# Last block of a two-layer model on one core: expert layer gathered by halves of the experts, and last tiles done one column half after the other

## What is computed

```python
def moe_swiglu(h, router, w_gate, w_up, w_down):
    ht = h.reshape(B * T, D)
    probs = jax.nn.softmax((ht @ router).astype(F32), axis=-1)
    top_p, top_i = lax.top_k(probs, TOP_K)                  # TOP_K = 2
    top_p = top_p / jnp.sum(top_p, axis=-1, keepdims=True)
    gates = jnp.sum(jax.nn.one_hot(top_i, N_EXPERTS, dtype=F32) * top_p[..., None], axis=1)
    out = jnp.zeros_like(ht)
    for e in range(N_EXPERTS):                              # 8 experts, hidden width 1536
        out = out + gates[:, e:e + 1] * swiglu(ht, w_gate[e], w_up[e], w_down[e])
    return out.reshape(B, T, D)
```

## Time and profile before

| | us |
|---|---|
| runs (3): lowest, median, highest | 1679.25, 1679.99, 1686.19 |
| the profiled execution: its own time | 1679.47 |
| its span | 1677.7 |
| TensorE busy in the span | 1612.0 |
| VectorE, ScalarE busy | 1166.4, 962.9 |
| weights and constants read, result written | 336.66 MB, 1.10 MB |

### The profile page before, as it was taken

How to read it: one execution, slowest core, us unless ns; L and a number is a source line. 1 busy time by engine, 2 the same in 40 slices (tenths; PEclk the granted TensorE clock), 3 DMA queues, 4 the chain that set the end, 5 groups by cost and what they waited for, 6 DMA issues and landing times.

```text
span 1677.7 us, 30052 instructions
## 1 busy us (share of the span) xinstructions
PE 1612.0 (96%) x11794; PEld 1435.0 (86%) x11794; DVE 1166.4 (70%) x1346; ACT 962.9 (57%) x1256; POOL 26.5 (2%) x37
## 2 busy tenths in 40 slices
PE   7999999999989999999999999999899999999997
PEld 6988999899879999899799998998678888888885
DVE  5677666644557666786755455867559888999885
ACT  6566455555565555754543445634357777777774
POOL 0000000000000000100000000200000000000000
PEclk9999999999999999999999999999889999999999
DMA  7535555434325555442345553631339999999993
GB/s 267 187 113 180 196 179 196 151 151 176 126 77 201 182 193 179 151 156 77 126 164 188 188 187 126 185 117 60 152 125 375 346 343 364 359 358 357 349 361 119
DMA packets 48225, 339.15 MB, mean 202 GB/s; under 512 B 5776, under 2 KB 5952, under 8 KB 8192
## 3 DMA queue, kind: packets, MB, share of 16 engines
q1 hardware_dynamic: 46064, 330.94, 53.4%
q0 software_dynamic: 2064, 6.83, 1.4%
HBM read 336.66 MB, written 1.10 MB: 201 GB/s over the span
## 4 chain that ended last, share of the span: by engine, by line
PE 53%; DVE 4%; ACT 3%; issue 1%; ACTq 0%; DVEq 0%
PE PS L1557 16%; PE PS L826 8%; PE PS L1575 8%; PE PS L1628 8%; PE PS L1645 4%; PE PS L1213 2%; PE PS L1512 1%; PE PS L1587 1%; DVE MWL L2463 1%; DVE ARENA L2846 1%; PE PS L1540 1%; PE PS L903 1%; ACT MWH L1785 1%; PE PS L1527 0%; ACT HN L1721 0%
## 5 line engine op out<-in xcount | busy, mean ns | idle before, releaser
L3050 DVE TENSOR_TENSOR EWL<-W,EWH 128x2048 fp32r<-128x2048 f32 x144 | 329.1, 2290 | 44.3 <-ACT EWH L2258 44.3
L2258 ACT ACTIVATE EWH<-W 128x2048 fp32r<-128x2048 f32 x144 | 276.2, 1919 | 67.5 <-PE PS L1575 36.7
L1628 PE MATMUL PS<-HTH,WH 128*128 128x256 f32 x1056 | 298.1, 282 | 5.3 <-DVE HTL L2435 5.3
L2458 DVE TENSOR_TENSOR WL<-W,WH 128x2048 fp32r<-128x2048 f32 x99 | 226.3, 2289 | 103.0 <-ACT WH L1767 102.0
L1628 PE MATMUL PS<-HTH,WL 128*128 128x256 f32 x1056 | 297.8, 282 | 0.0
L1628 PE MATMUL PS<-HTL,WH 128*128 128x256 f32 x1056 | 297.6, 282 | 0.0
L2463 DVE TENSOR_TENSOR MWL<-W,MWH 128x1024 fp32r<-128x1024 f32 x138 | 173.1, 1259 | 127.3 <-ACT MWH L1785 124.9
L1785 ACT ACTIVATE MWH<-W 128x1024 fp32r<-128x1024 f32 x138 | 144.7, 1055 | 167.8 <-PE PS L826 167.7
L1767 ACT ACTIVATE WH<-W 128x2048 fp32r<-128x2048 f32 x99 | 189.3, 1915 | 60.2 <-PE PS L1628 32.7
L1628 PEld LDWEIGHTS PS<-HTH,WH 128*128 128x128 f32 x1056 | 199.9, 189 | 7.0 <-issue 5.9
L1628 PEld LDWEIGHTS PS<-HTL,WH 128*128 128x128 f32 x1056 | 200.0, 189 | 1.0
(11 more groups left out here) (331 smaller groups left out, 2804.9 us busy)
## 6 DMA issues: line engine op xcount, KB each, us to landing
W<-in_weights SPq DMA_DIRECT2D x312, 1024.0 KB, 5.0
ARENA<-rows_m POOLq DMA_DIRECT2D x8, 192.0 KB, 5.4
ARENA<-rows_m POOLq DMA_DIRECT2D x2, 768.0 KB, 10.3
CS<-in_consts POOLq DMA_DIRECT2D x3, 403.0 KB, 4.3
X<-in_x SPq DMA_DIRECT2D x2, 512.0 KB, 3.6
out<-X SPq DMA_DIRECT2D x1, 1024.0 KB, 4.0
PR<-in_params SPq DMA_DIRECT2D x1, 830.0 KB, 7.7
CS<-in_consts POOLq DMA_DIRECT2D x2, 403.5 KB, 4.3
```

The lines of the kernel that those rows point to most:

```text
L1628: ins = mm(PS[b][:, c * 256:(c + 1) * 256], wt[:, sl, o:o + P], ht[:, kk, :], start=(kk == 0 and n == 0), stop=(kk == KC - 1 and n == 2))
L2258: A(EWH[tile % SPLIT][:, :], tile_ap(w0 + tile), ACT.Copy).then_inc(sem("moe_hi"), 1)
L2458: TT(WL[:, j % SPLIT, :], tile_ap(t), WH[:, j % SPLIT, :].bitcast(F32), SUB).then_inc(lo_done, 2)
L3050: TT(EWL[tile % SPLIT][:, :], tile_ap(w0 + tile), EWH[tile % SPLIT][:, :].bitcast(F32), SUB).then_inc(sem("moe_lo"), 1)
```

## The change

It has four parts. **Norms:** in front of mixers the table load goes behind the three splits; in front of FFNs the Silu load goes behind the evictions of the transposed rows. **Last tiles:** `out_last_tile` and the last `down` of an FFN finish one bank of y after the other. **Norm 7, router, gather:** HN is split a token tile at a time inside norm 7, two of four residual matmuls go between the transposes of the two token tiles, the router's first row of matmuls waits for each bank of HT by itself, SELR is made and the gather is run for experts 0 to 3 and then 4 to 7, evictions alternate between ScalarE and VectorE, and the transposes of SELR go behind chunks 2 to 5 of the second half. HNH and HNL move to other memory, so the first two expert tiles are split earlier. **End:** the last down tile is split ahead of the last group's Silu, the last turn goes inside the down before it, the last down, YH, YL and scatter run by column halves, the four copies are shared out, and the result leaves in four DMAs of 256 KB, with the branch for more tokens ahead of them.

```diff
@@ SyncE
-        for b in range(4):
-            await_free_of(sp, ("y", last_resid, b))
         if last_resid == "moe":
             with sp.If(more_tokens(sp) > 0):
...
-        sp.dma_start(out_dram.rearrange("b (t p) d -> p (b t) d", p=P), X[:, :, :]).then_inc(s_out, 16)
-        sp.wait_ge(s_out, 16)
+        out_tiles = out_dram.rearrange("b (t p) d -> p (b t) d", p=P)
+        for b in (0, 2, 1, 3):
+            await_free_of(sp, ("y", last_resid, b))
+            t, cols = b // 2, slice((b % 2) * 512, (b % 2 + 1) * 512)
+            sp.dma_start(out_tiles[:, t, cols], X[:, t, cols]).then_inc(s_out, 16)
+        sp.wait_ge(s_out, 64)
@@ TensorE, norm
                     if t == NT - 1:
                         done(ins, ("norm", n, b))
+                if n == 7 and t == 0:
+                    residual_in(moe_name[0], (0, 1))
@@ TensorE, out_last_tile
             for tt in range(NT):
-                for k, c in enumerate(chunks):
-                    for hf in range(2):
+                for hf in range(2):
+                    for k, c in enumerate(chunks):
                         ins = products(PS[2 * tt + hf][:, :], False, name, h + k, slice(hf * 512, (hf + 1) * 512), c,
                                        slice(tt * P, (tt + 1) * P), False, k == 1)
...
@@ TensorE, router
-            hT_ready(7)
...
             for t in range(NT):
-                for k in range(KC):
+                for j, b in enumerate((0, 2, 1, 3)):
+                    if t == 0:
+                        await_free_of(pe, ("norm", 7, b))
+                    for i, k in enumerate(NORM_CHUNKS[b]):
...
-            residual_in(moe_name[0])
+            residual_in(moe_name[0], (2, 3))
@@ TensorE, moe
-            pe.wait_ge(sem("hn_lo"), p + 1)
-            pe.wait_ge(sem("moe_sel"), p + 1)
-            for c in range(KC):
-                for hf in range(2):
+            pe.wait_ge(sem("hn_lo"), NT * (p + 1))
...
+            for hf in range(2):
+                pe.wait_ge(sem("moe_sel"), 2 * p + hf + 1)
+                for c in range(KC):
+                    key = ("moe", p, "gx", hf, c)
+                    claim(pe, key)
+                    for n in range(2):
+                        for t in range(NT):
+                            hn = HNL[t][:, c * P:(c + 1) * P] if n else HNH[:, t, c * P:(c + 1) * P]
+                            ins = mm(bank(key)[:, :], hn, SELR[:, t, 4 * hf:4 * hf + 4, :].rearrange("p e s -> p (e s)"),
+                                     start=(n == 0 and t == 0), stop=(n == 1 and t == NT - 1))
+                    done(ins, key)
+                    if hf and c in MOE_TURN_BEHIND:                 # (2, 3, 4, 5)
+                        turn_selection(MOE_TURN_BEHIND.index(c))
@@ TensorE, moe, down
+                        if gs == MOE_GROUPS - 2 and c == 1 and n == 0:
+                            turn(MOE_GROUPS - 1, 0)
...
+            def last_down():
...
+                for hf in range(2):
+                    for c in range(2):
+                        for n, (gh, w) in enumerate(((GRH, EWH), (GRH, EWL), (GRL, EWH))):
+                            if n == 2:
+                                pe.wait_ge(free[b], k0[b] + gs // 2 + 1)
+                            o = c * D + hf * 512
+                            ins = mm(PS[4 + hf][:, :], gh[:, gs % 2, c * P:(c + 1) * P], w[sl][:, o:o + 512],
+                                     start=False, stop=(c == 1 and n == 2), skip_group_check=True)
+                    ins.then_inc(w_used if hf else sem("moe_half"), 1)
...
+            def last_scatter():
+
+                for hf in range(2):
+                    for n, y in enumerate((YH[:, hf * 512:(hf + 1) * 512], YL[hf][:, :])):
+                        if n:
+                            pe.wait_ge(free[4 + hf], k0[4 + hf] + N_EXP)
+                        else:
+                            pe.wait_ge(sem("moe_yh_last"), 2 * p + hf + 1)
+                        for t in range(NT):
+                            ins = mm(PS[2 * t + hf][:, :], GS[:, t * P:(t + 1) * P], y, start=False, stop=(n == 1), skip_group_check=True)
+                            if n:
+                                done(ins, ("y", name, 2 * t + hf))
@@ TensorE, ffn, last down only: halves = ((0,), (1,)), else ((0, 1),)
                 for tt in range(NT):
-                    for c in range(2):
-                        for n, (gh, wt) in enumerate(((GHH, WH), (GHH, WL), (GHL, WH))):
-                            for hf in range(2):
+                    for hfs in halves:
+                        for c in range(2):
+                            for n, (gh, wt) in enumerate(((GHH, WH), (GHH, WL), (GHL, WH))):
+                                for hf in hfs:
@@ ScalarE, norm
             if n in mixer_of_norm and n:
+                feed(n)(SPLIT - 1)
                 logs()
-                feed(n)(SPLIT - 1)
...
-            if n in ffn_of_norm:
-                act.preload_act_table(ACT.Silu)
...
+            if n == 7:
+                normed_hi(0)
...
                 if n in ffn_of_norm:
+                    act.preload_act_table(ACT.Silu)
                     for k in range(EARLY, SPLIT):
                         hi(ffn_of_norm[n], k, 0)
...
+            normed_hi(1)                       # A(HNH[:, t, :], HN[:, t, :], Copy) behind both halves of HN
@@ ScalarE, moe
-            act.preload_act_table(ACT.Silu)
-            A(HNH[:, :, :].rearrange("p t d -> p (t d)"), HN[:, :, :].rearrange("p t d -> p (t d)"), ACT.Copy).then_inc(sem("hn_hi"), 1)
...
             hi(0, 0)
+            if not p:
+                router()
+            act.preload_act_table(ACT.Silu)
+            hi(1, 0)                           # behind the router's logits, before: behind the gather
...
@@ ScalarE and VectorE, moe, group: the split of the last down tile stands ahead of the last group's Silu
                 if gs < MOE_GROUPS - 1:
                     hi(moe_tile(gs + 1, "up0"), i)
+                else:
+                    hi(moe_tile(gs, "down"), i)
...
-            expert_out(N_EXP - 1, 0)
+            for hf in range(2):                # YH by halves; then y bank 1 to X on ScalarE
...
@@ VectorE, norm and router
+            if n == 7:
+                normed_lo(0, 0)
...
+            normed_lo(0, 1)                    # HNL[t] = HN[:, t] - HNH[:, t]
...
-            split_normed(0)
...
+            link(TT(mo.POS, mo.EX, bank(key)[:, 0:16], ADD))
+            select(0)
             link(dve.tensor_reduce(mo.MOST, bank(key)[:, 16:24], AX.X, MAX))
...
+            select(1)                          # select(hf): SELR of experts 4 hf to 4 hf + 3
@@ VectorE, moe
-            lo(0, 0)
-            for c in range(KC):
-                key = ("moe", p, "gx", 2 * c + 1)
+            for hf in range(2):
+                for c in range(1, KC, 2):
+                    key = ("moe", p, "gx", hf, c)
...
+                    if hf == 0 and c == 1:
+                        lo(0, 0)
+                    if hf and c == 1:
+                        stage(0, 0)
+                    if hf and c == 3:
+                        lo(1, 0)
...
-            for b in range(4):
+            for hf in range(2):                # YL by halves
...
+            for b in (0, 2, 3):                # copies to X
```

More of the change, by code:

```diff
@@ L437, in build @@
     moe_name = ["moe", "moe_more"]
+    MOE_TURN_BEHIND = (2, 3, 4, 5)
     def plan_moe(p):
@@ L473, in build @@
                 plan(("y", moe_name[0], b), b)
-            plan(("router", "place"), 5)
+            plan(("router", "place"), 7)
         elif st[0] == "moe":
@@ L1471, in mixer2, with residual_in @@
             out_last_tile(m, M2_OUT, M2_OUT_CHUNKS[-2:])
-        def residual_in(name):
-            for b in range(4):
+        def residual_in(name, banks=range(4)):
+            for b in banks:
                 claim(pe, ("y", name, b))
@@ L1503, in moe, with turn_selection @@
             w0, k0 = BASE["moe"] + p * MOE_TILES, ffn_k0[name]
-            pe.wait_ge(sem("hn_lo"), p + 1)
-            pe.wait_ge(sem("moe_sel"), p + 1)
-            for c in range(KC):
-                for hf in range(2):
[L1508 to L1516, removed]
+            pe.wait_ge(sem("hn_lo"), NT * (p + 1))
+            def turn_selection(j):
                 key = ("moe", p, "selT", j)
@@ L1577, in down, with scatter @@
                                      skip_group_check=True)
+                        if gs == MOE_GROUPS - 2 and c == 1 and n == 0:
+                            turn(MOE_GROUPS - 1, 0)
                 ins.then_inc(w_used, 1)
-            def scatter(e, i, last=False):
+            def last_down():
+                gs = MOE_GROUPS - 1
+                b, tile = 6 + gs % 2, moe_tile(gs, "down")
+                sl = tile % SPLIT
+                await_split(tile, 0)
+                pe.wait_ge(sem("moe_gh"), MOE_GROUPS * (p + 1))
+                for hf in range(2):
[7 more added lines that the diff above has]
```

(24 more changed lines are left out.)

124 lines of the change are left out of this document (74 added, 50 removed).

## The result

The changed kernel takes 1658.99 us, the median of 4 runs (1658.44 to 1660.66), against 1681.53 for the kernel before on the same chip (4 runs): a ratio of 0.9864, 95% interval 0.9851 to 0.9878, 22.9 us. The forecast was 1658.5. The profiled execution took 1660.66 with a span of 1658.8, so the sum 21.3 stands against 18.8 between the two profiles.

What follows compares the result with a forecast made beforehand. The prediction took TensorE, busy for 96% of the span, as the bound. Its terms, 2.9 + 0.8 + 4.5 + 2.5 + 2.5 + 8.1 = 21.3 us, gave 1658.2, or 1658.5 as a median; 8-in-10 range 1654 to 1664.

Steps and rivals of the forecast that it cites:

- Norms: Norms 1 to 6: earlier splits and banks gain 2.9 us before mixers, later Silu loads 0.8 before FFNs.
- The reordered last output tile gives nothing here: Norms 1, 3, 5: no gain from the reordered tile, as ScalarE is busy from first square to root.
- Gather start: Norm 7 and router to gather: earlier logits, placement and half of SELR start the gather 4.5 us sooner (3.4 to 5.5).
- Idle in front of the gate matmuls: Between gather and gate matmuls: TensorE's idle 2.55 us goes with SELR's turns inside the gather; gain 2.5 us.
- Gate matmuls: First gate matmuls: without idle time they begin at 2.4 GHz, taking 4.2 us instead of 6.75; gain 2.5.
- First up: First up tile after the gate matmuls: the clock may fall again, so nothing counted (0 to 1.9 us).
- End: Last down tile to output: earlier split, work by halves, earlier branch and four DMAs gain 8.1 us (6.9 to 9.0).
- the landing: Output DMA at the end: the last quarter lands in 2.8 us instead of the whole's 4.0; gain 1.2.
- (a): Gather: idle time returns as bank waits and gate matmuls fall back to 1.2 GHz; 1663 us, chance 0.13.
- (b): Gate matmuls and first up: both run at 2.4 GHz, 0.8 + 1.9 us more gained; 1655.5, chance 0.12.
- (c): Expert loop: the weight stream is the real limit, so only norms and end gain; 1667.7 us, chance 0.04.
- (d): Expert loop: the ring of six runs short and each of 48 groups waits; 1680 to 1685 us, chance 0.03.

Runs made afterwards that it cites:

- norms alone: The kernel before with only the new order of work in norms 1 to 6 and bank-by-bank last down and out tiles; 1675.08 us, ratio 0.9965.
- front alone: The kernel before with only norm 7, router, gather and the expert layer's first stages changed; 1671.40 us, ratio 0.9948.
- fill, gather alone: The changed kernel with six unread matmuls ahead of the gather and nowhere else; 1657.46 us, ratio 0.9854.

## Why the prediction came out right, step by step

- Norms, 3.7 predicted: 4.3 by stages in norms alone. Between the two profiles only 2.5 is seen, since that of after has a dip at 140 us, which the one of before hasn't. The mechanism was right; "The reordered last output tile gives nothing here" was wrong by 0.2 a norm, as norms 1 and 3 show.
- Gather start, 4.5 (3.4 to 5.5): 3.7 after, 5.4 in front alone, with the same code. The range's two ends were the two clocks, and both came up. The steps as written end at 1203.6 and not at 1203.8, which would have made the term 4.8, further from the 3.7.
- Idle in front of the gate matmuls, 2.5: gone, but not by the turns behind chunks 2 to 5 alone, which the prediction names. ScalarE's splits moved forward do it as well. The price was right, the cause half of it.
- Gate matmuls, 2.5: 2.9 (3.7 in place of 6.6 from start to start, 3.88 in place of 6.75 busy). That the idle time brings the fall of the clock forward is shown: with the idle back, 6.30. The fall comes at the end of the idle time or just behind it, not well inside.
- First up, 0: 0.5 after. It begins at 1.2 GHz in both, for 3.8 us before and 2.9 after.
- End, 8.1: 6.7 in both traces that allow it. Start of the last down tile 1.8 (1.9), down to last copy 4.0 (3.7), branch 1.15 (1.3): right. The mis-sized term is the landing: 1.2 predicted, -0.2 between the two profiles, 0.3 over all traces. By an estimate from the Trainium skill's formula (DMA: Bandwidth & Descriptors, "Anatomy of one DMA"), which the page fits to DMAs issued by GpSimd, an overlapping quarter would have landed 2.6 after the last issue. The trace of these, which SyncE issues, has 4.2, and the measurement decides.
- Rivals: (a) no waits in the gather, refuted. (b) the kinder clock came for the gate matmuls and not for the first up. (c), (d) refuted by the loop's windows.

Between the two profiles the misses are -1.2 (norms), -0.8 (gather start), +0.4 (idle), +0.4 (gate), +0.5 (up), -1.4 (end) and -0.3 (loop), together -2.4 of the 2.5 that 18.8 lacks to 21.3. The runs show 22.9, since the profile before was 2.1 us under its median and that of after 1.7 above: that the forecast met the median within 0.5 is partly luck.

## What to carry to other kernels

When a bank or buffer is late, list everything that stands in front of its eviction in that engine's queue: moving any of it may do what an elaborate reordering does. Read a latency that you want to cut from several profiles before you price the cut. Where TensorE must wait before wide matmuls, a few unread ones in the wait can keep its clock up: here six in a wait of 1.6 us made the stretch behind them 1.5 to 2.5 us shorter.

## What the runs showed of the hardware that was not expected

- TensorE's granted clock fell to 0.50 at different instructions in different executions of the same front (in the router's last matmuls in after, behind place in front alone). The Trainium skill (TensorE: Matmul & The Clock Gate, "What's actually happening") says of the start of a kernel that the number of slow matmuls varies from run to run. The traces show the same 1.2 ms into this one, place taking 0.37 or 0.57 a pair.
- With six unread matmuls, 1.58 us of work in a wait of 1.64, in front of the gather, the stretch from there to the gate matmuls is 16.4 to 16.5 us in three traces; in the seven without them and without the idle time it is 18.0 to 19.0.
- Four 256 KB output DMAs land in 2.2 to 4.3 us, the last of them in 4.1 to 4.3 every time; one of 1 MB took 4.0, 4.3, 4.7 and 5.1.
- ScalarE's first activation starts at 5.8 to 6.2 us in ten of 14 profiles, at 6.7 and 7.0 in two and at 8.3 in two (norms alone and fill, gather alone). It is not x that it waits for: x has landed by 5.7 in every trace. It is the first DMA of parameters, issued at 2.15 and landed at 5.7 to 6.1, and at 8.2 in the two late ones; the whole run is later by that.
